# Neighbourhood scores as two 128-row products on stacked high and low parts

## The reference

```python
z = einsum('bsd,de->bse', rms_norm(x, g), w_in)      # q, k, v of both head kinds, and a gate
# four heads of differential attention: two softmaxes over all 1024 keys each
# eight heads of 2-D neighbourhood attention on a grid of 16 rows x 64 columns, head size 64:
s = einsum('bhnqd,brnkhd->bhnqrk', q, k) * 64**-0.5   # keys: 8 rows x a window of 16 columns
s = where(valid, s + bias, -inf);  o = einsum('...', softmax(s), v)
x = x + einsum('bse,ed->bsd', concat(o_da, o_na) * silu(gate), w_out)
```

## Time and profile before

| what | value |
|---|---|
| median of 3 runs | 1434.71 us (1434.34 to 1435.35) |
| the profiled execution's own time | 1431.96 us |
| its span, first to last instruction | 1430.2 us |
| mean granted TensorE clock | 0.997 |
| PE busy | 1408.8 us, 99% of the span |
| DVE busy | 873.9 us, 61% |
| ACT busy | 692.3 us, 48% |
| POOL busy | 651.3 us, 46% |

### The profile page before, as it was taken

One profiled execution on the slowest core, in us unless ns is written; L12 is line 12 of the kernel. 1 busy time (PEld: TensorE's weight loads), 2 busy tenths in 40 slices (PEclk: granted clock), 3 DMA queues, 4 the chain that ended last, 5 costly groups with the idle time before them and its releaser, 6 DMA issues.

```text
span 1430.2 us, 23575 instructions
## 1 busy us (share of the span) xinstructions
PE 1408.8 (99%) x8068; PEld 1150.9 (80%) x8068; DVE 873.9 (61%) x1803; ACT 692.3 (48%) x1373; POOL 651.3 (46%) x488
## 2 busy tenths in 40 slices
PE   9999999999999999999999999999999999999996
PEld 7788887888888888778787888888888888887875
DVE  7767677677555555653437677767676555656333
ACT  6545555555444444642525554545554444456331
POOL 3223223234666666643642231323256666667152
PEclk9999999999999999999999999999999999999998
DMA  5700101121111111311110110100202111213113
GB/s 184 154 30 26 48 22 37 37 63 38 44 57 50 50 45 55 126 30 59 59 44 30 38 37 15 44 29 22 78 23 65 37 62 37 63 38 127 44 59 118
DMA packets 40698, 79.57 MB, mean 56 GB/s; under 512 B 18992, under 2 KB 19248, under 8 KB 40624
## 3 DMA queue, kind: packets, MB, share of 16 engines
q1 hardware_dynamic: 40480, 78.60, 17.6%
q10 hardware_dynamic: 144, 0.01, 0.0%
HBM read 66.57 MB, written 15.96 MB: 58 GB/s over the span
## 4 chain that ended last, share of the span: by engine, by line
PE 91%; POOL 2%; ACT 2%; DMA 2%; DVE 2%; issue 1%; SPq 0%; POOLq 0%; DVEq 0%; ACTq 0%
PE proj L1077 18%; PE proj L1079 17%; PE proj L1078 17%; PE scores L1113 12%; PE turn L1172 6%; PE mix L1223 3%; PE mix L1224 3%; PE scores L1172 2%; PE mix L1190 2%; PE mix L1189 2%; PE mix L1188 2%; DMA w_raw<-chunks 1%; POOL w_lo L658 1%; POOL prob L766 1%; PE mix L1198 1%
## 5 line engine op out<-in xcount | busy, mean ns | idle before, releaser
L1077 PE MATMUL proj<-h_hi,w_hi 128*128 128x512 f32 x1168 | 483.9, 414 | 3.4 <-POOL w_lo L658 2.7
L1079 PE MATMUL proj<-h_hi,w_lo 128*128 128x512 f32 x1168 | 458.7, 393 | 0.0
L1078 PE MATMUL proj<-h_lo,w_hi 128*128 128x512 f32 x1168 | 455.6, 390 | 0.0
L647 POOL TENSOR_TENSOR w_lo<-w_raw,w_hi 128x1024 fp32r<-128x1024 f32 x62 | 152.9, 2466 | 309.9 <-ACT w_hi L847 309.9
L1589 DVE TENSOR_TENSOR pt_lo<-turn,pt_hi 128x512 fp32r<-128x512 f32 (+1 forms) x208 | 139.1, 669 | 207.3 <-ACT pt_hi L889 206.0
L1079 PEld LDWEIGHTS proj<-h_hi,w_lo 128*128 128x128 f32 x1168 | 219.2, 188 | 49.8
L1077 PEld LDWEIGHTS proj<-h_hi,w_hi 128*128 128x128 f32 x1168 | 220.1, 188 | 45.1 <-issue 5.2
L1078 PEld LDWEIGHTS proj<-h_lo,w_hi 128*128 128x128 f32 x1168 | 220.8, 189 | 34.8
L889 ACT ACTIVATE pt_hi<-turn 128x512 fp32r<-128x512 f32 (+1 forms) x208 | 120.4, 579 | 200.4 <-PE turn L1172 200.1
L698 POOL TENSOR_SCALAR prob<-prob,rrec 128x512 f32<-128x512 f32 (+1 forms) x96 | 157.1, 1648 | 113.0 <-DVE rrec L1614 112.5
L1581 DVE CUSTOM_DVE_ANT_0 prob<-scores,inner 128x1024 f32<-128x1024 f32 (+1 forms) x192 | 203.5, 1060 | 3.2 <-PE scores L1113 2.7
(11 more groups left out here) (189 smaller groups left out, 2311.5 us busy)
## 6 DMA issues: line engine op xcount, KB each, us to landing
w_raw<-chunks SPq DMA_DIRECT2D x80, 512.0 KB, 3.5
mixed_dram<-gate SPq DMA_DIRECT2D x28, 256.0 KB, 2.4
edge<-bias_dram SPq DMA_DIRECT2D x32, 224.0 KB, 4.8
h_lo<-mixed_dram SPq DMA_DIRECT2D x14, 512.0 KB, 6.8
xt<-x_t SPq DMA_DIRECT2D x8, 512.0 KB, 8.0
out_t<-xt SPq DMA_DIRECT2D x16, 256.0 KB, 2.1
bias_dram<-bias_rows SPq DMA_DIRECT2D x16, 240.0 KB, 6.2
dist_dram<-inner SPq DMA_DIRECT2D x1, 480.0 KB, 6.5
```

The lines of the kernel that those rows point to most:

```text
L647: pool.tensor_tensor(w_lo[:, b], w_raw[:], f32(w_hi[:, b]), ALU.subtract).then_inc(w_lo_done, 1)
L1077: pe.matmul(dst, a_hi, b_hi, start=start, stop=False)
L1078: pe.matmul(dst, a_hi, b_lo, start=False, stop=False)
L1079: return pe.matmul(dst, a_lo, b_hi, start=False, stop=stop)
```

## The change

In the NA groups the head's high and low parts are stacked on the partitions. For head 0, `k_hi` holds the keys' high part on partitions 0 to 63 and their low part on 64 to 127; for head 1, `k_lo` holds the low part on 0 to 63 and the high part on 64 to 127. ACT and DVE write these as two instructions of 64 rows and 1024 columns each, where each had one of 128 rows.

For each tile and head, `q_hi` receives a stack of 128 x 128 with the queries' high part on both halves (ACT: four copies of 64 x 128 for a tile, `stack_hi_part`), and `q_lo` one with the low part on the head's own half and zeros on the other (DVE: two subtractions of 64 x 128, `stack_lo_part`). A product of 128 rows with the first gives `q_hi k_hi + q_hi k_lo`, with the second `q_lo k_hi`. So a tile of 512 keys is 4 matmuls of 128 rows, and an inner tile is 8, in spans of 384 and 192 columns. There are four slots for stacks. The zeros are written once in a layer by DVE (`clear_stacks`), after the low keys of the first NA group.

POOL's `q_lo_part` and ACT's 512-column copy are gone for the NA groups. The raw queries stay in `q_next` (first half) and in `k_next[:, 512:]` (second half). DVE makes the stack of the next group's tile 0 in step 7 ahead of `k_lo_part`, that of tile 1 at the start of step 8, those of tiles 2 and 3 at the start of step 1, and then one in each of the steps 2 to 5. ACT makes the high stacks of tiles 0, 1, and 2 with 3 in steps 6, 7 and 8, and then one in each of the steps 1 to 4, ahead of lines 929 and 930.

```diff
+    SPANS = [[[(0, 384), (384, 576)], [(0, 192), (192, 576)]] if INNER[t] else [[(0, HALF)]] * 2 for t in range(NT)]
+    STACKS = 4
...
+        def stacked_hi(g, behind, t):
+            if behind and behind.na and t >= NT - 2:
+                return [(behind, i) for i in ([0], [1], [2, 3])[t - (NT - 2)]]
+            return [(g, t + 3)] if g.na and t < NT - 3 else []
+        def stacked_lo(g, behind, t):
+            if behind is not True and behind and behind.na and t >= NT - 1:
+                return [(behind, t - (NT - 1))]
+            return [(g, i) for i in ([2, 3] if t == 1 else [t + 2])] if g.na and t < NT - 2 else []
...
-                act.activation(k_hi[:], k_next[:], ACT.Copy).then_inc(k_hi_done, 1)
+                if g.to_na:
+                    for m in range(2):
+                        last = act.activation(k_stack[m][own(m)], k_next[own(m)], ACT.Copy)
+                    last.then_inc(k_hi_done, 1)
...
+            def stack_hi_part(g, t):
+                act.wait_ge(qk_done, g.step(t) - 3)
+                act.wait_ge(piece_freed, g.piece(0) - (TILE[True][t] < NT // 2))
+                for m in range(2):
+                    for to in range(2):
+                        last = act.activation(stack(q_hi, t, m)[own(to)], raw_queries(t)[own(m)], ACT.Copy)
+                last.then_inc(stack_hi, 1)
...
+                if g.na:
+                    if t == 0:
+                        pe.wait_ge(stack_zero, 2 * (g.l + 1))
+                    pe.wait_ge(stack_lo, g.tiles(t) + 1)
+                    first = KEY0[t] * W
+                    for m in range(2):
+                        for a, b in SPANS[t][m]:
+                            out = all_scores[:, window(t, m) + a:window(t, m) + b]
+                            keys = k_stack[m][:, first + a:first + b]
+                            pe.matmul(out, stack(q_hi, t, m), keys, start=True, stop=False)
+                            last = pe.matmul(out, stack(q_lo, t, m), keys, start=False, stop=True)
+                    last.then_inc(qk_done, 1)
+                    return
...
+            def stack_lo_part(g, t):
+                dve.wait_ge(stack_hi, g.tiles(t) + 1)
+                for m in range(2):
+                    rows = own(m)
+                    last = dve.tensor_tensor(stack(q_lo, t, m)[rows], raw_queries(t)[rows], f32(stack(q_hi, t, m)[rows]),
+                                             ALU.subtract)
+                last.then_inc(stack_lo, 1)
+            def clear_stacks(g):
+                dve.wait_ge(qk_done, g.l * (GROUPS * NT) + DA_G * NT)
+                for m in range(2):
+                    part = q_lo[own(1 - m), :].rearrange("p (s m c) -> p s m c", m=2, c=P)[:, :, m]
+                    dve.memset(part.bitcast(F32), 0.0).then_inc(stack_zero, 1)
+            def k_lo_part(n, to_na=False):
                 dve.wait_ge(k_hi_done, n + 1)
+                if to_na:
+                    for m in range(2):
+                        last = dve.tensor_tensor(k_stack[m][own(1 - m)], k_next[own(m)], f32(k_stack[m][own(m)]),
+                                                 ALU.subtract)
+                    last.then_inc(k_lo_done, 1)
+                    return
...
+                for to, i in stacked_lo(g, behind, t):
+                    stack_lo_part(to, i)
                 if g.project and t == NT - 1:
-                    k_lo_part(g.group() + 1)
+                    k_lo_part(g.group() + 1, g.to_na)
+                    if g.to_na and not g.na:
+                        clear_stacks(g)
```

More of the change, by code:

```diff
@@ L154, in __init__ @@
             self.g = i + (DA_G if na else 0)
+            self.to_na = na or (isinstance(i, int) and i == DA_G - 1)
         def step(self, t):
@@ L176, in group, with tiles, queries @@
             return self.l * GROUPS + self.g
+        def tiles(self, t):
+            return (self.l * NA_G + self.i) * NT + t
+        def queries(self, hf):
+            return 2 * (self.l * DA_G + self.i) + hf
         def order(self):
@@ L302, in prob_of, with stack, raw_queries, own @@
             return prob[:, 2 if m else t % 2, first:end]
+        k_stack = (k_hi, k_lo)
+        def stack(buf, t, m):
+            at = (2 * (t % STACKS) + m) * P
+            return buf[:, at:at + P]
+        def raw_queries(t):
+            tile = TILE[True][t]
+            part = k_next[:, HALF:] if tile >= NT // 2 else q_next[:]
+            return part[:, tile % 4 * P:(tile % 4 + 1) * P]
+        def stacked_hi(g, behind, t):
[6 more added lines that the diff above has]
+            return [(g, i) for i in ([2, 3] if t == 1 else [t + 2])] if g.na and t < NT - 2 else []
+        def own(m):
+            return slice(m * HD, (m + 1) * HD)
         def pair_cols(na, t):
@@ L417, in hybrid_encoder @@
         inner_ready = sem("inner_ready")
-        tail_done = sem("tail_done")
+        stack_hi = sem("stack_hi")
+        stack_lo = sem("stack_lo")
+        stack_zero = sem("stack_zero")
         qk_done = sem("qk_done")
@@ L744, in attend @@
                         normalise(g, (t - 3) // 2)
-                    if front and front.projects(ft) and ft // 2 == Q_:
+                    if front and front.projects(ft) and ft // 2 == Q_ and not front.to_na:
                         q_lo_part(front, ft)
@@ L874, in piece_part @@
                     act.activation(gate_tanh[:], gate[:, cols], ACT.Tanh).then_inc(piece_half, 1)
-                if kind == Q_:
+                if kind == Q_ and g.to_na:
+                    act.nop().then_inc(piece_half, 1)
+                elif kind == Q_:
                     act.wait_ge(piece_freed, g.freed(t) + 1)
@@ L992, in attend @@
                             piece_part(g, t)
+                    for to, i in stacked_hi(g, behind, t):
+                        stack_hi_part(to, i)
                     for i in rows[1]:
@@ L1102, in score @@
                     pe.wait_ge(k_lo_done, g.group() + 1)
[L1103 to L1114, removed]
@@ L1130, in score @@
+                if t == 0:
+                    pe.wait_ge(q_ready, g.queries(0) + 1)
+                if t == STEP0[False]:
+                    pe.wait_ge(q_ready, g.queries(1) + 1)
+                tile = slice(TILE[False][t] * P, (TILE[False][t] + 1) * P)
+                for cols in (slice(0, HALF), slice(HALF, S)):
                     for p in range(3):
                         for m in range(2):
[L1132 to L1135, removed]
+                            out = all_scores[:, m * S + cols.start:m * S + cols.stop]
+                            last = pe.matmul(out, (q_hi, q_lo, q_hi)[p][own(m), tile], (k_hi, k_hi, k_lo)[p][own(m), cols],
+                                             start=p == 0, stop=p == 2)
@@ L1544, in piece_part @@
                         dve.wait_ge(k_lo_done, g.group() + 1)
+                    if t % 2 and g.na:
+                        dve.wait_ge(stack_lo, g.tiles(NT))
+                    if t % 2 and isinstance(g, First) and g.l:
+                        dve.wait_ge(stack_lo, g.l * NA_G * NT)
                     dve.tensor_tensor(k_next[:, cols], ps, rbc[:, cols], ALU.mult).then_inc(piece_freed, 1)
```

19 lines of the change are left out of this document (13 added, 6 removed).

## The result

The changed kernel takes 1470.9 us, median of 4 runs (1469.4 to 1474.3), against 1434.5 for the kernel before on the same chip (4 runs, 1431.4 to 1435.4): ratio 1.026, interval 1.024 to 1.028. It is 36.4 us slower, where I had forecast 8.5. The direction was right, the time lies far outside the range.

A forecast was written before the change was run, and what follows sets the result against it. PE bounds the kernel: its gain of 13.1 us (0.6 swallowed) against waits of 12.3, 3.0, 3.0 and 3.2 gives +9.0, a median of 1443.7 us, stated as 1443; range 1436.5 to 1449 (8 in 10).

The forecast's parts named there:

- PE's gain: PE at NA scores: 128-row matmuls save 0.15 us per 512-key tile and 0.25 per inner tile, 13.1 us in all.
- the rule and the rows in the forecast: PE's 512-key tiles: by the skill's row-tiling rule 32 tiles lose 7.4 us; by the profile rows they gain 4.8.
- The new instructions alone: ACT and DVE preparation: four copies 1.28 us, two short differences 0.61, the keys' low part in two halves 2.46.
- rival (a): 64-row instructions on ACT and DVE take half the time, so waits total 4.2 us: 9 us faster, 1426; 5%.
- Waits at tile 0 and tile 2: PE waits for stacks and keys: 12.3 us between NA groups, 3.0 from DA to NA, 3.0 at tile 2.
- The last group, 2 times: Each layer's last group: ACT's copies delay DVE's read of tile 3's scores, tile 4's scores wait; 1.6 us each, 3.2.
- (d): Rival: more waits than found, say in `weigh`, where DVE's splits end last; above 1449 us; 8%.

The follow-up runs named there:

- the version with all moves: Changed kernel with low keys earlier, POOL's weights held back, last group's stacks at step ends, tile 2's stack before output pair: 1431.4 us, 0.9983 of the kernel before.

## Why the prediction was wrong

- **PE's gain**: mechanism right, size too large: 10.6 for 13.1 us (0.11 and 0.21 a tile for 0.15 and 0.25). From the projection ahead of the scores to the transposes it is 1.17 us at a 512-key tile and 1.39 at an inner one, where the sum had 1.14 and 1.36; over 64 tiles that is 1.9 of the 2.5 us. The 64-row blocks' gaps do go; the DA scores of the changed kernel, still 64 rows, keep their 0.33 us on either side:

```profile
343.44 0.40 PE L1139 MATMUL proj<-h_hi,w_lo 128*128 128x512 f32 x1
343.77 0.50 PE L1185 MATMUL scores<-k_hi,q_hi 64*128 64x512 f32 x2
344.11 0.39 PE L1185 MATMUL scores<-k_hi,q_lo 64*128 64x512 f32 x2
```

  Of the rule and the rows in the forecast, the rows were right: the Trainium skill's case for two row tiles ("TensorEngine Tiling (Array Packing)", When to Use Tiling) would have made the 512-key tiles slower, and they are faster.
- **The new instructions alone**: right. Pair 0.58 for 0.61, copies 1.27 for 1.28, keys 2.44 for 2.46; no 64-row instructions overlapped, so rival (a) is out. The Trainium skill ("ScalarE: Activation LUTs", What ACT_TABLE_LOAD costs) gives copies an overlap of about 93 ns; by that four would take some 0.28 us less, and the traces have 1.25 to 1.27 us, which the rows had given without it.
- **Waits at tile 0 and tile 2**: right in place and cause. That the sum fits too (18.3 us) is in part luck: 11.9, 3.8 and 2.6 for 12.3, 3.0 and 3.0, with errors that cancel.
- **"The last group, 2 times"**: this step failed. I took 0.30 us for a short difference from rows where POOL was quiet, and priced only ACT's copies and one late read, 1.6 us. Beside POOL each such difference waited for the end of an instruction of up to 2.4 us, and the pair stood ahead of the splits that PE needs. 23.9 us instead of 3.8 (half clock behind these waits contained); putting the pair elsewhere gave 15.3 back. What remains in the version with all moves, 3.3 us in the first layer, is still above the 1.9 a layer that I had forecast for ACT's copies; two pairs still meet POOL there (2.24 and 1.74 us), and I didn't separate the two causes.
- **The evidence was there.** The low keys took 1.47 us at the earlier trace rows beside POOL and 1.22 without, and I carried this as a small spread of a price. It was the tail of POOL's instruction: the excess is bounded by what is left of that, not by the 0.25 us seen. One of the 16 low keys of the kernel before, which I didn't look up behind the mean of 1.36, has it in full:

```profile
737.99 2.58 DVE L1560 TENSOR_TENSOR k_lo<-k_next,k_hi 128x1024 fp32r<-128x1024 f32 x1 [1.34 <-ACT k_hi L885]
737.09 2.40 POOL L647 TENSOR_TENSOR w_lo<-w_raw,w_hi 128x1024 fp32r<-128x1024 f32 x1 [8.88 <-ACT w_hi L847]
```

  It ends 1.08 us after POOL's instruction, as the one of 1.47 does. The Trainium skill says so ("SBUF — State Buffer", Who interferes with whom): a VectorE instruction with two SBUF inputs contends with a GpSimd one that reads SBUF. Another section of that page of the Trainium skill (SBUF: two separate sides) adds that the one to start first keeps the shared ports and "the other fully blocks". The traces agree, with 0.58 grown to 3.44 us, and with u<-mix,u, which has one input in PSUM, staying at 0.42 and 0.43 beside the same POOL work. I cited other pages and not this one.
- **The clock**: not in the sum at all. 4.8 us at three group starts, and by the estimate above up to 6.4 behind the last groups' waits.
- **The rivals**: what happened is (d), more waits than I found, at 8%. Its sentence named the releaser, DVE's splits, but not the place (the transposes, not `weigh`); I didn't look at what DVE's queue would meet there.

## What to carry to other kernels

Price a two-input DVE instruction that is moved or added by what POOL does in that stretch, not by its length: lay both queues side by side before choosing the place, and ask what stands behind it. A wait of PE costs its own length and, now and then, a stretch at half clock behind it, so that filling it with useless matmuls can pay, and removing it pays more than its length. When a change brings a gain on the bounding engine and loses it in preparation, look for another order before giving it up: here the same instructions ran at +36 and at -3 us.

## What the runs showed of the hardware

- A DVE instruction with two SBUF inputs that meets a POOL TENSOR_TENSOR ends a nearly fixed time after it: 0.14 to 0.25 us for 64 x 128, 1.07 to 1.09 for 1024 columns (two that began in the same moment as POOL's got through). Between two such POOL instructions in a row exactly one gets through. POOL's TENSOR_SCALAR (lines 728 and 739) held up none by more than 0.41 us: a pair begun under it took 0.58 or 0.99. It depends on when: the 81 short differences of all traces that began 0.16 to 0.31 us after the start of such an instruction took 0.63 to 0.70 us and ended 0.74 to 0.75 before it did; the 260 that began 0.80 us or more after its start took 0.27 to 0.29. By the words of the Trainium skill's page ("SBUF — State Buffer", Who interferes with whom), it reads SBUF and should block as well; the traces show this for the first part of the instruction alone.
- Six matmuls of no use, 1.4 us in a wait of 1.9, kept the granted clock at 1.00. Without them, it fell to 0.50 behind a wait of 1.7 to 1.9 us at some group starts and not at others, and at different ones from run to run: at one to five of eight, 18 of 48 in six traces. What decides that stays open.
- Matmuls of 128 rows and 192 columns start 0.09 to 0.12 us apart at PE, those of 128 columns 0.11, and those of 384 columns 0.18.
